# A decoder layer on eight cores: second pass of the first channel mixer over its weight pieces in reverse, two pieces kept on chip

## The reference, cut to what matters

```python
def swiglu(h, w_gate, w_up, w_down):
    return (jax.nn.silu(h @ w_gate) * (h @ w_up)) @ w_down
...
h = modulate(rms_norm(x, norm_ffn1[l]), sh1, sc1)
x = x + 0.5 * gt1[:, None, :] * swiglu(h, ffn1_w_gate[l], ffn1_w_up[l], ffn1_w_down[l])
h = modulate(rms_norm(x, norm_mix[l]), sh2, sc2)
x = x + gt2[:, None, :] * hybrid_mixer(h, w_in[l], ...)
h = modulate(rms_norm(x, norm_ffn2[l]), sh3, sc3)
x = x + 0.5 * gt3[:, None, :] * swiglu(h, ffn2_w_gate[l], ffn2_w_up[l], ffn2_w_down[l])
```

## Time and profile before

| | us |
|---|---|
| median of 3 runs (lowest, highest) | 2379.86 (2378.62, 2387.29) |
| the profiled execution's own time | 2381.77 |
| its span (core 6, the slowest) | 2380.2 |
| the eight cores' spans | 2356.7 to 2380.2 |
| PE busy, share of the span | 2245.6, 94% |
| DVE, ACT, POOL busy | 1089.4, 608.9, 518.0 |
| share of PE in the chain that ended last | 85% |

### The profile page before, as it was taken

The page is one execution under the profiler, slowest core; times in us unless marked ns, Lnnn a source line. Parts: engine busy times, 40 slices in busy tenths (PEclk is TensorE's granted clock), DMA queues, the critical chain, the costliest instruction groups (busy, mean ns, idle before and its releaser), DMA issues.

```text
span 2380.2 us, 31984 instructions; the slowest of 8 cores (2356.7 to 2380.2 us)
## 1 busy us (share of the span) xinstructions
PE 2245.6 (94%) x11300; PEld 1046.6 (44%) x11524; DVE 1089.4 (46%) x1856; ACT 608.9 (26%) x1045; POOL 518.0 (22%) x632
## 2 busy tenths in 40 slices
PE   3899999997899999899999999999999999999999
PEld 1444444443344444444544545444444444434444
DVE  1254543455444444344445444766434444454443
ACT  2501011142111111145666666211122111111111
POOL 2120201134211210133535535400011202010100
PEclk9999999998999999999999999999999999999999
DMA  9553634369646633466342445751211515042302
GB/s 179 127 70 47 87 56 54 39 157 209 79 58 89 89 53 90 67 159 67 48 47 32 57 45 69 104 62 18 58 46 48 104 34 80 10 67 32 54 36 106
DMA packets 260587, 174.50 MB, mean 73 GB/s; under 512 B 172112, under 2 KB 239824, under 8 KB 258512
## 3 DMA queue, kind: packets, MB, share of 16 engines
q0 software_dynamic: 152336, 135.82, 36.9%
q1 hardware_dynamic: 108096, 36.62, 8.4%
HBM read 221.56 MB, written 20.97 MB: 102 GB/s over the span
## 4 chain that ended last, share of the span: by engine, by line
PE 85%; DMA 5%; issue 2%; SPq 2%; ACT 2%; DVE 2%; POOL 2%; another core or an unknown queue 0%; DVEq 0%; ACTq 0%; POOLq 0%
PE ps L215 85%; SPq L215 2%; DMA Dw<-ffn_w_up 2%; DMA B<-C 1%; ACT Dw L215 1%; DMA B<-B 1%; DVE A L215 1%; POOL C L215 1%; ACT C L215 1%; POOL rstd L215 0%; DMA A<-Dw 0%; ACT A L215 0%; DVE E L215 0%; DVE Dw L215 0%; DVE C L215 0%
## 5 line engine op out<-in xcount | busy, mean ns | idle before, releaser
L215 PE MATMUL ps<-B,Dw 128*128 128x512 bf16 x6000 | 1371.4, 382 | 57.2 <-DVE B L215 16.8
L215 PEld LDWEIGHTS ps<-B,Dw 128*128 128x128 bf16 x6144 | 596.9, 98 | 761.4 <-issue 83.0
L215 DVE TENSOR_TENSOR A<-ps,A 128x512 f32<-128x512 f32 (+2 forms) x764 | 478.2, 644 | 182.1 <-PE ps L215 175.7
L215 ACT ACTIVATE E<-ps 128x512 f32<-128x512 f32 x296 | 176.4, 596 | 1329.3 <-PE ps L215 1302.4
L215 DVE TENSOR_TENSOR E<-ps,E 128x512 bf16<-128x512 f32 (+1 forms) x288 | 199.0, 691 | 661.3 <-PE ps L215 641.5
L215 PE MATMUL ps<-Dw,E 128*128 128x512 bf16 x2003 | 463.2, 380 | 16.3 <-DVE A L215 11.5
L215 PEld LDWEIGHTS ps<-Dw,E 128*128 128x128 bf16 x2048 | 195.7, 98 | 269.4 <-issue 46.5
L215 ACT ACTIVATE Dw<-ps 128x512 bf16<-128x512 f32 (+2 forms) x280 | 163.3, 588 | 264.9 <-PE ps L215 260.2
L215 POOL DMA_DIRECT2D Dw<-ffn_w_gate x70 | 50.2, 718 | 538.3 <-PE ps L215 537.6
L215 PE MATMUL ps<-B,C 128*128 128x512 bf16 x503 | 120.3, 379 | 0.5
L215 POOL TENSOR_TENSOR Dw<-Dw 128x256 bf16<-128x256 bf16 (+1 forms) x128 | 101.3, 795 | 63.3 <-ACT Dw L215 49.5
(11 more groups left out here) (95 smaller groups left out, 1091.8 us busy)
## 6 DMA issues: line engine op xcount, KB each, us to landing
Dw<-ffn_w_down POOLq DMA_DIRECT2D x66, 256.0 KB, 6.5
Dw<-w_in POOLq DMA_DIRECT2D x60, 256.0 KB, 7.0
Dw<-ffn_w_gate POOLq DMA_DIRECT2D x56, 256.0 KB, 4.9
Dw<-ffn_w_up POOLq DMA_DIRECT2D x56, 256.0 KB, 5.3
C<-w_ada POOLq DMA_DIRECT2D x24, 512.0 KB, 9.1
A<-xo POOLq DMA_DIRECT2D x4, 2048.0 KB, 10.9
x1s<-A POOLq DMA_DIRECT2D x4, 2048.0 KB, 6.7
A<-x1s POOLq DMA_DIRECT2D x4, 2048.0 KB, 9.5
```

The source lines that it names most:

```text
L215: ins = getattr(engine, name)(*a, **kw)
```

## The change

Four edits:

1. Pass 1 takes the pieces in reverse order. Its first two pieces (numbers 6 and 7) are then the last two of pass 0 (5 and 4), which already lie in the slots with their down weights scaled: nothing is loaded or scaled for them.
2. `slot` numbers the slots back from the turn on, and `flip` of the first channel mixer goes from 0 to 1, with the opening's loads and the first block of modulation weights in exchanged slots. The last piece of pass 1 ends in the same slot as before.
3. `settle` of `n2[1, tg]` is 18.0 for all tiles.
4. `late2` is called after unit 1.

```diff
-    blk = [Dw[:, 12288:20480].rearrange("p (k n) -> p k n", k=KC),
+    blk = [Dw[:, 0:8192].rearrange("p (k n) -> p k n", k=KC),
...
-            wide_load(SV[0][j][:, :, c], f1[j][:, c], (nm, "s", half))
+            wide_load(SV[1][j][:, :, c], f1[j][:, c], (nm, "s", half))
...
-            for q, (j0, nj) in enumerate(PIECES):
+            for q, (j0, nj) in enumerate(PIECES[::-1] if pi else PIECES):
                 seq.append((pi, q, w, gi, j0, nj))
+        NP = len(PIECES)
+        slot = lambda p: ((p if p < NP else 2 * NP - 1 - p) + flip) % 2
...
         def load(p, what):
-            if p >= len(seq):
+            if p >= len(seq) or NP <= p < NP + 2:
                 return
             pi, q, w, gi, j0, nj = seq[p]
-            s = (p + flip) % 2
+            s = slot(p)
...
-            if i == 2 and late is not None:
+            if i == 1 and late is not None:
                 late(load)
...
-    run(load_d(f1, 0, *PIECES[0], False))
+    run(load_d(f1, 1, *PIECES[0], False))
...
-        run(scale_task(0, 4, 0))
+        run(scale_task(1, 4, 0))
...
-            n2[1, tg] = Norm("n2", 0.0 if tg == 3 else 1.5, tg, xn_c[tg % 2], 3, 16, 24, None, None, None, tg == 3, 18.0 if tg == 3 else 11.0)
+            n2[1, tg] = Norm("n2", 0.0 if tg == 3 else 1.5, tg, xn_c[tg % 2], 3, 16, 24, None, None, None, tg == 3, 18.0)
...
-    ffn([(f1, 0), (f1, 0)], pre, post_all, None, 0, gates, last=log_table)
+    ffn([(f1, 0), (f1, 0)], pre, post_all, None, 1, gates, last=log_table)
```

More of the change, by code:

```diff
@@ L621, in ffn @@
                 u = Unit()
-                u.p, u.pi, u.q, u.tg, u.s, u.nj, u.hb, u.gi = p, pi, q, tg, (p + flip) % 2, nj, len(units) % 2 + (2 if gates is not None and p == 0 and tg >= 2 else 0), gi
+                u.p, u.pi, u.q, u.tg, u.s, u.nj, u.hb, u.gi = p, pi, q, tg, slot(p), nj, len(units) % 2 + (2 if gates is not None and p == 0 and tg >= 2 else 0), gi
                 units.append(u)
         def load(p, what):
-            if p >= len(seq):
+            if p >= len(seq) or NP <= p < NP + 2:
                 return
             pi, q, w, gi, j0, nj = seq[p]
-            s = (p + flip) % 2
+            s = slot(p)
             if what == 0:
```

## The result

| | before | after |
|---|---|---|
| median of four runs (lowest, highest), us | 2381.57 (2378.62, 2387.29) | 2349.13 (2348.68, 2351.14) |
| the eight cores' spans in the profiled run | 2356.7 to 2380.2 | 2335.4 to 2347.1 |
| mean of the eight spans | 2370.1 | 2341.6 |
| read from HBM, MB | 221.56 | 208.98 |

The ratio is 0.9863, with an interval from 0.9842 to 0.9883: 1.4% or 32 us faster, and the prediction said 2352. The kernel before has one run more here than in the first table.

The account below looks back on a forecast made before the run. PE, busy 94% of the span, bounds the kernel; only its waits and the slow clock after them can be gained. 15.6 + 7.7 + 0 + 5.9 = 29.2 off core 6's 2380.2, plus 1, gives 2352; range 2345 to 2364.

Parts of the forecast that it names:

- Part 1: Between the passes, pass 1 backwards with two pieces kept: the 20.6 us loss falls to 5, gain 15.6 (11.6 to 20.4).
- The earlier meeting: Same load, transposes and write two tiles earlier, no weight load near: transposes ready 15.5 and 19.8 us after load, loss 9.0.
- the short wait is sure: Between the passes: PE's 2.6 us wait for an emptying of PSUM stays; the fall of the clock is not sure.
- Part 2: Before the token mixer, modulation at 18 instead of 11: the stall in `down` goes, gain 7.7 us (4 to 7.7).
- Core 4 gains nothing from parts 1 and 2: Core 4 would gain only 5.9 us, from 2356.7 to 2350.8, and might then be the slowest core.
- Cost at the mixer's start: The third tile's modulation now comes behind the fourth's scaling, ending near 1066.5: taken as 0, between -1 us and nothing.
- the third rival: Slower: cores fall into step and meet at memory around 1003, 1096 and 1910, 39 us more; time 2397, chance 0.03.
- Part 3: Second channel mixer, second piece's loads one unit sooner: PE's wait for the last gate load goes, gain 5.9 us (4.1 to 5.9).
- The greatest of eight: Allowance of 1 us because another core may be the slowest, giving a span of 2352.
- The first: Rival: between the passes the 2 MB load and the write hold the transposes, not the weights; sum 18.1, time 2363, chance 0.16.
- The second: Rival: the later modulation still waits, the stall moves into `gu`, gain 2 instead of 7.7 us; time 2357, chance 0.06.
- a wait of PE over 5 us appears after 1000 that was not there: Sign set beforehand, for the trace after 1000 us, that the whole prediction would be wrong.

Follow-up runs that it names:

- the second profile: The changed kernel run once more, unchanged, beside the version with moved w_in loads on the same chip: 2351.12 us, ratio 0.9853.

## Why the prediction was right

**The bound.** Right: the waits and the clock after them were what could be gained; PE's busy time on core 6 fell by 9.4 of 2245.6 us (0.4%), nearly all of it where the clock rose, and the other 24.9 of 34.3 us were idle time.

**Part 1.** Right in mechanism. The earlier meeting served as a gauge: forecast ready times of 15.5 and 19.8 us after the load came as 14.3 and 18.7. The remaining loss on core 6 was put at 5 between 0 and 9.0 and came as 2.8, so the gain is 17.8 for 15.6. (The upper bound of that gain, written as 20.4, is 20.6 by its own sum.) The step that was a little off is "the short wait is sure": C<-C came 14.3 us after the load where it had come 15.9 after it before, so the wait shrank from 2.6 to 0.8 and did not bring the clock down. The run with the piece loaded again shows the cause, not only the coincidence. Some luck was in the size: the second profile has a core on which the 2 MB load alone brought back 6.8 us of wait, which the forecast did not allow for.

**Part 2.** Right: 7.7 forecast for core 6, 7.7 measured, with no stall moved into `gu`. "Core 4 gains nothing from parts 1 and 2" was wrong in its second half: core 4 lost 4.4 us there too (47.6 to 43.2), which I had not looked up. It changed the candidate for the slowest core (core 4 at 2350.8), not the sum.

**Cost at the mixer's start.** I put 0, between -1 and 0; core 6 went from 59.3 to 60.7, the mean of the cores from 56.7 to 58.9. The edit itself isn't the cause: with `settle` alone the stretch stays at 56.7. The wait that grew is one that I had not named, behind the transposes of v, and no run shows why it is longer with all parts together. How much longer it is, is itself uncertain: the changed kernel's second profile has a mean of 57.9, with that wait at 3.3 to 7.6 us. It may be the third rival in small: the cores now leave pass 1 nearer to each other, so their w_in loads coincide more. The run with the piece loaded again, whose cores are apart, has 57.1, which fits, but was not made to test it.

**Part 3.** Right: 5.9 forecast, 5.9 measured on core 6 by the same 96 matmuls. Missed was the 1.1 us behind it (sooner scaling of the down weights).

**Smaller terms.** The edit's rest was put at nothing; pass 1 has 1.2 us less on all cores. The greatest of eight was taken as 1 us above the sum; in fact the spread narrowed, and core 6 fell by 34.3, not 29.2: 31.3 from the three parts in their stretches and 2.3 in the two long ones, less 1.4 at the mixer's start; the other 2.1 are differences of either sign elsewhere, the largest of them 2.6 before PE's first weight load. So the forecast lies 3 us above the result, inside its range.

**The rivals.** The first (load and write hold the transposes, 2363) fell: the write was issued at 581.41 as it said, near 582, but B<-C was ready 0.55 us after it, not 15.4. The rule of turns beneath it holds; what it missed is that the transposes were through by then, since no weight load had slowed them. The second (the modulation still waits, 2357) fell on all cores. The third (in step, 2397) fell as a whole: the first of its three meetings got shorter, and it wanted 7.2 us more at each. But the sign "a wait of PE over 5 us appears after 1000 that was not there" was not clean. The wait behind the transposes of v was there on every core and passed 5 us on four more of them (cores 1, 2, 3 and 5: 3.4 to 3.9 before, 6.5 to 7.9 after; core 6: 5.6 and 7.4). It took back 2.2 us of the mean, so the whole was right, and the sign was drawn too tight.

## What to carry to other kernels

Where a kernel waits for transposing DMAs, look at what else was issued in those microseconds, and ask first what of it need not be moved at all: a second pass that starts at the end where the first stopped finds its operands on chip. Moving the same loads to another time pays only where they aren't then late for their own use; the later w_in loads had such room, the weight loads held back had not. An earlier meeting of the same transfers in the same trace, without the suspect, was a good price list here for the meeting without it. Before giving a stream of transfers a larger share, count how many packets it needs: three times a small share can still be next to nothing. When a stall of varying length is removed on eight cores, the slowest core can gain more than the mean (here 33.1 and 28.4 us), since its time also held the bad luck of the meeting.

## What the runs showed of the hardware

Two queues on the same DMA engines moved equal or nearly equal numbers of packets while both had work (136 and 135, 377 and 377 in 4 us; 64 and 50 in the earlier trace rows) whatever the sizes, 1.48 MB against 0.03 in one case; but tripling the small queue's share did not shorten what waited on it, for alone it moved 3652 packets in 4 us. A 2 MB load took 9.4 to 11.3 us on eight cores and 16.5 in one case, with nothing of its own core's beside it but the transposes and a write. Two transposing DMAs of v took 8.6 us beside w_in loads and 4.9 alone. And short gaps of PE need not bring its clock down: with gaps of 0.5 to 0.8 us it stayed at 1.00, the 2.4 GHz level, where waits of 2.6 and 15.3 us in the same place had left a mean of 0.87.
